# An mLSTM stage with tokens on the partitions, and its convolution and gate rows inside the input product

## What is computed

```python
qk = silu(causal_dwconv(concat([m_q, m_k]), conv_w, conv_b))       # 4 taps
ig, logf = m_i + i_bias, log_sigmoid(m_f + f_bias)                 # one row per head
b    = cumsum(logf)
m_t  = max over s <= t of (b[t] - b[s] + ig[s])                    # and the carried state
sc   = (q @ k.T) * 64 ** -0.5 * exp(dmat - m_t)                    # causal
h    = (sc @ v) / maximum(abs(sum(sc)), exp(-m_t))
h    = sigmoid(m_o) * rms_norm(h, mlstm_norm)                      # per head over its 128 values
```

## Time and profile before

| | us |
|---|---|
| median of 3 runs (lowest, highest) | 3762.57 (3760.34, 3766.36) |
| the profiled execution, its own time | 3759.47 |
| span of its profile | 3757.6 |
| TensorE matmul / weight load / VectorE / ScalarE / GpSimd busy | 3365.8 / 2359.3 / 1935.9 / 1489.5 / 562.7 |

### The profile page before, as it was taken

The page is one execution under the profiler, slowest core; times in us unless marked ns, Lnnn a source line. Parts: engine busy times, 40 slices in busy tenths (PEclk is TensorE's granted clock), DMA queues, the critical chain, the costliest instruction groups (busy, mean ns, idle before and its releaser), DMA issues. The chain is left out here.

```text
span 3757.6 us, 38218 instructions
## 1 busy us (share of the span) xinstructions
PE 3365.8 (90%) x13472; PEld 2359.3 (63%) x13472; DVE 1935.9 (52%) x2317; ACT 1489.5 (40%) x1918; POOL 562.7 (15%) x304
## 2 busy tenths in 40 slices
PE   7976699999899979597999897799999999999976
PEld 6742465887545558465888544577676777777752
DVE  2046533334424450425003324788888888888835
ACT  3223123443234433113223101566666666565623
POOL 3400002444100024212445100000000000000010
PEclk9966659999999989799999997899999999999988
DMA  3220501222121112121222611899999999999940
GB/s 135 107 90 34 190 1 67 93 108 90 68 83 52 67 45 90 67 90 45 93 108 90 271 67 70 361 398 401 400 401 398 402 404 396 406 395 405 396 191 23
DMA packets 69955, 713.67 MB, mean 190 GB/s; under 512 B 7408, under 2 KB 7792, under 8 KB 29424
## 3 DMA queue, kind: packets, MB, share of 16 engines
q1 hardware_dynamic: 58704, 670.10, 45.1%
q0 software_dynamic: 7056, 25.69, 1.7%
q10 hardware_dynamic: 4112, 16.78, 1.1%
HBM read 672.17 MB, written 40.37 MB: 190 GB/s over the span
## 5 line engine op out<-in xcount | busy, mean ns | idle before, releaser
L136 POOL TENSOR_TENSOR ring_low<-ring,ff_ring_high 128x1024 fp32r<-128x1024 f32 x136 | 331.5, 2471 | 924.0 <-ACT ff_ring_high L131 924.0
L197 PE MATMUL psum<-ff_high,ff_ring_high 128*128 128x512 f32 x832 | 326.0, 392 | 23.2 <-DVE h_low L337 8.6
L199 PE MATMUL psum<-ff_high,ring_low 128*128 128x512 f32 x832 | 325.3, 391 | 0.0
L197 PE MATMUL psum<-ex_high,ex_rows_high 128*128 128x512 f32 x768 | 316.3, 412 | 6.8 <-DVE ring_low L2359 6.8
L199 PE MATMUL psum<-ex_high,ex_rows_low 128*128 128x512 f32 x768 | 301.8, 393 | 0.0
L198 PE MATMUL psum<-h_low,ff_ring_high 128*128 128x512 f32 x704 | 275.1, 391 | 0.0
L2359 DVE TENSOR_TENSOR ex_more_low<-ex_more,ex_high_in_x 128x2048 fp32r<-128x2048 f32 x96 | 219.5, 2286 | 70.4 <-ACT ex_high_in_x L2286 70.4
L2359 DVE TENSOR_TENSOR ring_low<-ring,ex_high 128x2048 fp32r<-128x2048 f32 x96 | 214.3, 2287 | 40.3 <-ACT ex_high L2286 40.3
L1338 PE MATMUL psum<-h,ring 128*128 128x512 f32 x512 | 224.0, 594 | 1.1 <-ACTq L1409 1.1
L2248 PE MATMUL psum<-ex_more,ex_act_t 128*128 128x512 f32 x512 | 224.9, 592 | 0.0
L2286 ACT ACTIVATE ex_high<-ex_more 128x1024 fp32r<-128x1024 f32 x192 | 200.5, 1062 | 57.4 <-PE psum L199 57.4
(11 more groups left out here) (508 smaller groups left out, 6703.7 us busy)
## 6 DMA issues: line engine op xcount, KB each, us to landing
ex_more<-moe_w SPq DMA_DIRECT2D x128, 2048.0 KB, 9.7
ring<-wstream SPq DMA_DIRECT2D x87, 2048.0 KB, 8.1
ring<-moe_w SPq DMA_DIRECT2D x64, 2048.0 KB, 12.0
ex_bias_up<-moe_b SPq DMA_DIRECT2D x32, 1024.0 KB, 8.5
y_rows<-ex_y SPq DMA_DIRECT2D x33, 512.0 KB, 9.2
y_rows<-mx_zero ACTq DMA_DIRECT2D x1, 16384.0 KB, 51.8
ex_bias_down<-moe_b SPq DMA_DIRECT2D x32, 512.0 KB, 8.4
x<-xt SPq DMA_DIRECT2D x8, 256.0 KB, 5.7
```

What stands on the lines that cost most here:

```text
L136: e.tensor_tensor(low, full, high.bitcast(F32), ALU.subtract).then_inc(self.low_ready, 1)
L197: pe.matmul(out, a[0], b[0], start=start, stop=False)
L199: return pe.matmul(out, a[1], b[0], start=False, stop=stop)
```

## The change

1. **Order of panels.** The panel with ik, i, f and iw becomes panel 3; i, f and iw are laid out with i on 32 columns, f on 32 and iw behind them, so that one tile of 72 columns has all three. VectorE takes it in three copies. aq, ak, av and iq follow as panels 4 to 7.
2. **Convolution inside the input product.** ScalarE makes the base straight from the tile's bank into the (still unused) iq buffer, VectorE adds the three taps from the bank, which is its take of the tile, and ScalarE's Silu writes qk. The two iq takes by VectorE wait for the four Silus.
3. **Gate rows inside the input product.** ScalarE's five steps stand behind its tiles 15 to 18, VectorE's five (two scans) behind its tiles 20 to 24. The silu of c stands at tile 7. The cumulative sum is a scan with add and min in one.
4. **mLSTM with tokens on the partitions.** The weights (keys on the partitions) become the stationary operand and the values, with a 129th column of ones, the moving one: 10 products of 128x129 a head give numerator and denominator with tokens on the partitions. exp is taken from the spread row with `a` as its bias; only the diagonal pieces go through VectorE, which adds `a` and caps with a constant that is 0 or -1e30, so the mask is gone. The square is summed along the free dimension by ScalarE. One root of 128x4 and one reciprocal of 128x4 give both divisions: h = num * (sum(num^2)/128 + eps * den^2)^-1/2. ScalarE scales the numerator while it copies, TensorE turns it back (four transposes), and VectorE multiplies with norm weight and gate in one step. Spreads and scores of head h+1 are issued ahead of the turn of head h.
5. **Modulation.** EARLY goes from 3 to 4: panels 0 and 1 ahead of head 0's products, panels 2 and 3 behind head 1's scores. The index stage has eight panels left.
6. **iw** is turned onto the partitions in the mLSTM stage; the floor is taken once, for all heads, as exp(-m) of 128x16.

The core of the diff:

```diff
 class Modulation:
-    EARLY = 3
+    EARLY = 4
...
+class Rows:
...
+    def act_step(self, act, i, tile_ready, dve_took, bank):
+        if i == 7:
+            act.wait_ge(self.cond_ready, 1)
+            act.activation(self.cond[:, :, 0:1].rearrange("p k a -> p (k a)"), g.cols[:, COLS.at["c2"]:COLS.at["c2"] + DT], ACT.Silu)\
+                .then_inc(self.cond_ready, 1)
+        if i < 4:
+            act.wait_ge(tile_ready, i + 1)
+            act.activation(b1["iq"][:, i, :], bank, ACT.Identity, scale=col("conv_w", 3 * 4 + i),
+                           bias=col("conv_b", i)).then_inc(self.based, 1)
+        if 4 <= i < 8:
+            act.wait_ge(dve_took, i - 3)
+            act.activation(b1["qk"][:, i - 4, :], b1["iq"][:, i - 4, :], ACT.Silu).then_inc(self.qk_ready, 1)
+        if i == 15:
...
+    def convolve(self, dve, i, bank):
+        dve.wait_ge(self.based, i + 1)
+        for tap in (2, 1, 0):
...
+            done = dve.scalar_tensor_tensor(to, bank[:, 0:S - back], col("conv_w", tap * 4 + i), to, ALU.mult, ALU.add)
...
 def mlstm_stage(g, b1, rows, mix, mo):
+    EXT = M_DV + 1
+    AT, ORDER = (0, S, S + 512, S + 384), (0, 1, 3, 2)
...
+            def _(act):
+                def weights(h):
+                    act.wait_ge(limited, TT * (h + 1))
+                    for j in ORDER:
+                        act.activation(part, part, ACT.Exp).then_inc(weighted, 1)
+                        if j < TT - 1:
+                            act.activation(prob[:, b, AT[j] + P:AT[j] + S - P * j], max_bank[:, P * (j + 1):S], ACT.Exp,
+                                           bias=a_col[:, j, h:h + 1]).then_inc(weighted, 1)
...
+                weights(0)
+                for p in range(2):
+                    act.wait_ge(panel_done, 4 * (p + 1))
+                    mo.take(act, p, psum[:, 4 + p, :]).then_inc(row_ready, 1)
+                for h in range(MH):
+                    if h == 0:
+                        weights(1)
+                        for p in range(2, 4):
+                            act.wait_ge(panel_done, 4 * (p + 1))
+                            mo.take(act, p, psum[:, 4 + p, :]).then_inc(row_ready, 1)
+                    elif h + 1 < MH:
+                        weights(h + 1)
+                    for i in range(TT):
+                        act.wait_ge(nd_done, TT * h + 2 * (i // 2) + 2)
...
+                        act.activation(junk[:, i % 2, :], num(h, i)[:, 0:M_DV], ACT.Square,
+                                       accum_out=squares[:, TT * h + i:TT * h + i + 1]).then_inc(squared, 1)
+                    act.wait_ge(den_ready, 4 * h + 4)
+                    act.activation(den[:, at], den[:, at], ACT.Sqrt).then_inc(std_ready, 1)
+                    act.wait_ge(inverted, h + 1)
...
+                    for i in range(TT):
+                        act.activation(scaled_num[:, q, i, :], num(h, i)[:, 0:M_DV], ACT.Copy,
+                                       scale=inv[:, TT * h + i:TT * h + i + 1]).then_inc(scaled, 1)
...
+            def _(pe):
...
+                for h in range(MH):
+                    if h + 1 < MH:
+                        spread_of(h + 1)
+                    if h == 0:
+                        pe.wait_ge(row_ready, 2)
+                    if h == 1:
+                        pe.wait_ge(row_ready, 4)
+                    if h:
+                        turn(h - 1)
+                    if h >= 2:
+                        pe.wait_ge(mixed, h - 1)
+                    products(h)
+                    if h + 1 < MH:
+                        scores_of(h + 1)
+                    if h == 0:
+                        pe.wait_ge(floor_ready, 1)
+                        for p in range(2, 4):
+                            mo.product(g, pe, p, psum[:, 4 + p, :], panel_done, p + 1)
+                turn(MH - 1)
```

More of the change, by code:

```diff
@@ L791, in mlstm_stage @@
[L791 to L795, removed]
+        a_col, floor = sb("a_col", [P, TT, MH]), sb("floor", [P, TT, MH])
@@ L848, in _, with spread_of @@
             @block.tensor
             def _(pe):
-                pe.wait_ge(cond_ready, 2)
-                for p in range(mo.EARLY):
-                    mo.product(g, pe, p, psum[:, 1 + p, :], panel_done, p + 1)
-                pe.wait_ge(rows_ready, 2)
+                def spread_of(h):
+                    if h:
+                        pe.wait_ge(weighted, 7 * h)
+                    pe.matmul(max_bank, g.neg_head[:, h, :], rows.max_row[:, :], start=True, stop=True).then_inc(spread, 1)
@@ new lines, in products, with turn @@
+                def products(h):
+                    for i in range(TT):
+                        pe.wait_ge(prob_ready, 3 * h + min(i, 2) + 1)
+                        for j in range(i + 1):
+                            at = AT[j] + (i - j) * P
+                            mm = pe.matmul(num(h, i), prob[:, h % 2, at:at + P], b1["mv"][:, j, h, :], start=j == 0, stop=j == i)
+                        mm.then_inc(nd_done, 1)
+                def turn(h):
+                    pe.wait_ge(scaled, TT * (h + 1))
+                    for i in range(TT):
+                        mm = pe.transpose(turn_bank(h)[:, i * P:(i + 1) * P], scaled_num[:, h % 2, i, :], g.ident)
+                    mm.then_inc(turned, 1)
@@ new lines, in _ @@
+                spread_of(0)
+                for j in range(TT):
+                    mm = pe.matmul(psum[:, 6, MH * j:MH * j + MH], rows.m_row[:, j * P:(j + 1) * P], g.ident[0:MH, 0:MH],
+                                   start=True, stop=True)
+                mm.then_inc(mcol_psum, 1)
+                for j in range(TT):
+                    mm = pe.matmul(psum[:, 5, IH * j:IH * j + IH], b1["raw"][64:64 + IH, j * P:(j + 1) * P],
+                                   g.ident[64:64 + IH, 64:64 + IH], start=True, stop=True)
@@ L1232, in block_1 @@
             for m in range(4):
-                to = b1[name][:, m, :]
                 e = "act" if m % 2 or name == "o_gate" else "dve"
-                take = copy[e](to) if name != "o_gate" else \
-                    (lambda to: lambda a, bank: a.activation(to, bank, ACT.Sigmoid))(to)
-                tiles.append(Tile([n0 + p], 0 if tokens else m * P, PANEL if tokens else P, h, to, e, take,
-                                  tokens=m if tokens else None, halves=(high, g.h_low)))
-        last = [n0 + 7]
@@ L1248, in block_1 @@
+                tiles.append(Tile([n0 + p], 0 if tokens else m * P, PANEL if tokens else P, h, None, e, take,
+                                  tokens=m if tokens else None, halves=halves))
         dense_stage(g, "in1", tiles, n0 + 8 + SLOTS, split_to=n0 + 8, dve_lows=True,
                     norm=lambda sem, scratch: Norm(g, sem, "n1", x, h, scratch, EPS_RMS, lambda t: col("norm_mix", t), centre=False,
-                                                   high=high, low=g.h_low))
+                                                   high=high, low=g.h_low), rows=rows)
```

341 lines of the change are left out of this document (187 added, 154 removed).

## The result

| us | before | after |
|---|---|---|
| median (lowest, highest) | 3761.45 (3760.01, 3766.36) | 3669.84 (3667.01, 3672.39) |
| the profiled execution, its own time | 3759.47 | 3667.01 |
| span of its profile | 3757.6 | 3665.2 |
| mean granted TensorE clock | 0.926 | 0.937 |
| TensorE matmul / VectorE / ScalarE busy | 3365.8 / 1935.9 / 1489.5 | 3304.2 / 1898.1 / 1486.3 |

The changed kernel takes 0.9754 of the time of before, 95% interval 0.9737 to 0.9771. The forecast was 3678.0, range 3658 to 3699.

What follows compares the result with a forecast made beforehand. Three stages of block 1 run in sequence, bound by TensorE, a three-engine chain per mLSTM head, and modulation panels. Savings 17.8 + 60.8 + 6.0 = 84.6 us; 3759.5 - 84.6 = 3674.9, plus 3.1 to the median: 3678, range 3658 to 3699.

Steps and rivals of the forecast that it cites:

- Input product: Block 1's first stage: 21.8 us of tiles gone, 0.4 for a longer last copy and 3.6 of waiting added, sum -17.8.
- the stall: Input product: the short panel, moved to fourth, does not cover its successor's load; a tile ends at 111.4, +3.6 us.
- Opening: mLSTM stage before head 0's products: transposes, spreads, scores and panels 0 and 1, 17 us, between 10.7 and 20.6 by clock.
- First head: mLSTM stage: products, next scores, panels 2 and 3 take 13 us; then head 0's squares, roots and turn 6.2.
- Two periods of 9: mLSTM stage, from head 1's products to head 3's: two periods of 8 or 12 us, taken as 9 each, 18.
- Products 3 and tail: End of the mLSTM stage: head 3's products 3 us, then small steps, turn and mixing 5.4.
- Index stage: Eight modulation panels instead of nine: the last take comes earlier, -6.0 us.
- A: Rival: low clock all through the mLSTM stage, 76.4 us in place of 62.6, total 3692; chance 0.25.
- B: Rival: high clock nearly all through the mLSTM stage, 50.2 us, total 3666; chance 0.17.
- C: Rival: mLSTM products of 129 columns are dear; at 1.2 us more per pass the total is 3774; chance 0.02.
- D: Rival: mLSTM path differs, removed work was beside it or panels land later (10, not 8.2): -70 or less, 3693 up; 0.08.
- The rule on table loads: mLSTM heads: a 1.38 us drain per ScalarE table switch would add some 11 us; the sum kept 1.28 per load.

Runs made afterwards that it cites:

- late_rows: The changed kernel with convolution, gate rows and cond column back at the head of the mLSTM stage: 3687.95 us, ratio to before 0.9804.
- idx_panels: The changed kernel with modulation panels 2 and 3 moved from the first head into the index stage's wait for the normed keys: 3661.82 us.
- short_last: The changed kernel with aq, ak and iq cut so that panel 3 has four tiles and the last panel two: 3669.34 us, again 3670.87.
- early3: The changed kernel with three early modulation panels in place of four, nine in the index stage: 3670.89 us, ratio to before 0.9762.
- wide_fill: Unused score products filling TensorE's waits ahead of the turns, added to the changed kernel with an extra 128x512 reciprocal per head: 3687.25 us.

## Why the prediction was right, point by point

Against the profiled execution the sum said 84.6 us and 92.5 came (3759.47 to 3667.01). The signs and places of all terms were right; the sizes were off by 7.9, of which 6.6 in the mLSTM stage.

- **Input product, -17.8:** -18.2. The tile of the short panel was forecast to end at 111.4; VectorE takes it at 111.20. The o_gate takes before it are 0.5 earlier (90.70 against 91.23), so the stall was a little longer than forecast, 3.85 us in place of 3.6. The convolution and the rows at no cost: shown by late_rows and the unchanged steps. The two table loads stand beside TensorE's passes at 128.46 and 141.13, as said.
- **Opening, 17:** 15.1 (195.33 to 210.44). The high level lasted beyond the start of the stage and came back before the end of the opening: panels 0 and 1 took 5.52 us together, not 6.6, and the spread behind them 1.1, not 1.9.
- **First head, 13 + 6.2 = 19.2:** 19.0 (210.44 to 229.42). Panel 3's landing bounds it, with 2.87 us of waiting, and head 0's squares stand behind its take (223.86, 224.35), as said. That the 13 fits (13.4, from 210.44 to the take at 223.86) is partly luck. It was chosen between the two clocks, with the transfer as a lower bound of 10.1 by a landing of 8.2 us. TensorE was at the high clock up to the wait, and it was the transfer that took longer: panel 1's product ends at 209.5, and panel 3's starts at 220.73, 11.3 us later, while the DMA moved about two panels (388 GB/s from 209 to 219). idx_panels shows what the two panels cost here: 10.9 us between products(0) and the turn of head 0, gone when they are.
- **Two periods of 9 = 18:** 14.95 (229.42 to 244.37; 7.60 and 7.35). This is the step that was mis-sized most. The 9 was chosen between "8 or 12", the 8 being ScalarE's work. ScalarE was the bound, but its work is 6.94 us: four squares with their sums take 1.1 to 1.2 us (224.35 to 225.49), where the sum had 1.9. Its own terms for ScalarE (1.7, 2.6, 1.9, 0.2 and 1.05) add up to 7.45 and were rounded to "about 8". The rest is the clock, which I had let decide the choice: it stood at the high level from 232 on. Where the profile has a lower clock in these heads the periods were 9.0 and 7.5 (short_last).
- **Products 3 and tail, 3 + 5.4 = 8.4:** 7.0 (244.37 to 251.34). No exp follows head 2's root, so the last root needs no table load (248.25, behind VectorE's step and not behind a load); the sum had counted one, 0.4 us longer than VectorE's steps beside it. 0.6 more is the products at the high clock, 2.4 in place of 3.
- **Index stage, -6.0:** -6.6. By early3 the price is also known, 6.1 us in the first head. The prediction named 6.2 for it, but by the wrong steps: squares, root and turn come behind a take with three early panels too, and what the fourth adds is its own wait and product, which the sum had inside the 13. The fourth early panel by itself is no gain that can be told.
- **Rivals.** A, low clock all through (3692): refuted, 0.50 stands in a third of the stage and 1.00 from 232 to its end. B, high clock nearly all through (3666), came nearer in its number than the forecast, but not for its reason: the stage took 56.0, the middle of 50.2 and 62.6, with both levels in it. C, dear products of 129 columns: refuted, 2.40 us for 20 passes. D, another path: its -70 or less did not come; the stage alone gave 67.4, more than forecast. Its other half, a longer landing, did come, and longer than the 10 us it named; it cost nothing against the forecast, since the 13 of the sum had room for it.
- **The rule on table loads.** Each load takes 1.28 us and the root starts 0.02 us behind it (225.50, 226.80), the next load 0.02 us behind the copies (227.25 + 1.14, 228.41). The Trainium skill, "ScalarE: Activation LUTs", section "What ACT_TABLE_LOAD costs", adds a drain of about 1.38 us to a switch; no row here shows one, and the sum was right to leave it out.

## What to carry to other kernels

When a chain runs from engine to engine, size each engine's queue per round from rows, and take the longest as the period; here it was ScalarE's with two table loads, and a 128x512 reciprocal put on that chain cost its 3.35 us and 1.3 more. Work moved ahead "because it has to be done anyway" is only free where the engine waits: two panels in the first head cost 10.9 us there; moved into the wait for the keys, where TensorE had nothing else to do, they gained 9.8 us in the median, though the index stage grew by 3.3. A gain of 3 us in one stage can be right in its place and not to be found in the median; read it at the stage's end, and again at the end of the stages behind it.

## What the runs showed of the hardware that was not expected

- The granted level in the heads does not follow TensorE's idle time in them in a simple way: 0.50 was granted from 231 to 236 in wide_fill with the engine busy throughout and for nearly 9 us before, and 1.00 from 232 to 252 in the changed kernel with 13.1 of 20 us busy. The same products took 2.40 to 2.50, 3.35 to 3.91, or 4.45 to 4.67 us by the level. What sets it was not settled.
- The same kernel's profiles differ: the mLSTM stages of the changed kernel by 0.4 us, the stretch behind the index stage by 4.9 (3322.9 to 3327.8).
- Small steps on the chain are short: 0.16 us for a step on 128x4 and 0.20 to the next one's start, 0.18 for the reciprocal, 0.25 from square to square of 128x128 with its sum read out.
